# The first job of a hybrid attention layer in units of 2 chunks and 256 tokens

## What is computed

```python
h = concatenate([meta, x], axis=1)                    # 16 learned tokens + 512, width 1024
h = layer_norm(h, ln_emb_g, ln_emb_b)                 # over the 1024 features
proj = h @ w_in                                       # split into 11 parts:
(qa, ka, va, ga, qi, ki, wi, cq, ckv, kpe, gb) = split(proj)
# branch A: indexer scores from qi, ki, wi; top 128 keys per query; softmax with T5 bias
# branch B: latent attention, q from rms_norm(cq) @ w_uq, k and v from rms_norm(ckv) @ w_ukv
mixed = concatenate([oa * silu(ga), ob * silu(gb)])
out = layer_norm(ALPHA * h + mixed @ w_out, ln_post_g, ln_post_b)[:, 16:]
```

## Time and profile before

| | us |
|---|---|
| median of 3 runs (range) | 334.42 (333.64 to 335.16) |
| the profiled execution | 335.0 |
| its span, first to last instruction | 333.2 |
| TensorE busy | 319.4 (96%) |
| VectorE, ScalarE, GpSimd busy | 235.9, 174.6, 199.2 |

### The profile page before, as it was taken

One profiled execution on the slowest core, in us unless ns is written; L12 is line 12 of the kernel. 1 busy time (PEld: TensorE's weight loads), 2 busy tenths in 40 slices (PEclk: granted clock), 3 DMA queues, 4 the chain that ended last, 5 costly groups with the idle time before them and its releaser, 6 DMA issues.

```text
span 333.2 us, 6144 instructions
## 1 busy us (share of the span) xinstructions
PE 319.4 (96%) x2098; PEld 275.9 (83%) x2098; DVE 235.9 (71%) x626; ACT 174.6 (52%) x382; POOL 199.2 (60%) x240
## 2 busy tenths in 40 slices
PE   8799999999999999989999999999999999999990
PEld 7588987778787888878797988897978898998990
DVE  5784720259965699999995995478787866564686
ACT  4685754343543355467545664677587753722220
POOL 6260899988432251556633589699859582660552
PEclk9799999999999999999999999999999999999998
DMA  7455432428513033202400232222323110130033
GB/s 270 190 147 223 131 94 95 128 74 296 176 63 127 1 107 100 79 0 73 136 2 16 65 129 97 91 77 92 98 92 95 66 35 30 66 126 2 2 122 130
DMA packets 11710, 32.86 MB, mean 99 GB/s; under 512 B 2409, under 2 KB 2793, under 8 KB 11681
## 3 DMA queue, kind: packets, MB, share of 16 engines
q1 hardware_dynamic: 8944, 26.89, 23.7%
q10 hardware_dynamic: 2736, 5.59, 5.5%
HBM read 29.83 MB, written 4.81 MB: 104 GB/s over the span
## 4 chain that ended last, share of the span: by engine, by line
PE 82%; DVE 10%; issue 2%; DMA 2%; ACT 2%; SPq 1%; DVEq 0%
PE ps_j L1319 50%; PE ps_o L1579 6%; PE ps_s L1530 4%; PE ps_s L1534 3%; DVE iw L1146 3%; PE ps_t L1319 3%; PE ps_s L1503 2%; DVE top L1142 2%; PE ps_t L1549 2%; DMA iw<-in_onehot 2%; PE ps_j L1371 2%; PE ps_t L1554 2%; ACT pr L910 1%; PE ps_j L1419 1%; PE ps_j L1382 1%
## 5 line engine op out<-in xcount | busy, mean ns | idle before, releaser
L569 POOL TENSOR_TENSOR wl<-raw,wh 128x1024 fp32r<-128x1024 f32 (+2 forms) x33 | 78.1, 2374 | 56.9 <-ACT wh L576 56.8
L1319 PE MATMUL ps_j<-hh,wh 128*128 128x512 f32 (+2 forms) x216 | 75.2, 348 | 0.1
L1319 PE MATMUL ps_j<-hl,wh 128*128 128x512 f32 (+2 forms) x216 | 74.7, 346 | 0.0
L1319 PE MATMUL ps_j<-hh,wl 128*128 128x512 f32 (+2 forms) x216 | 74.4, 345 | 0.0
L705 POOL TENSOR_SCALAR pr<-pr,rden 128x528 f32<-128x528 f32 (+1 forms) x64 | 35.3, 572 | 42.5 <-DVE rden L1186 42.5
L1319 PEld LDWEIGHTS ps_j<-hh,wh 128*128 128x128 f32 (+1 forms) x216 | 40.3, 186 | 6.3 <-issue 0.5
L1319 PEld LDWEIGHTS ps_j<-hh,wl 128*128 128x128 f32 (+1 forms) x216 | 40.3, 187 | 5.1
L1319 PEld LDWEIGHTS ps_j<-hl,wh 128*128 128x128 f32 (+1 forms) x216 | 40.3, 186 | 5.1
L910 ACT ACTIVATE pr<-pr,mn 128x528 f32<-128x528 f32 (+1 forms) x64 | 36.0, 564 | 14.4 <-DVE mn L1175 14.3
L576 ACT ACTIVATE wh<-raw 128x1024 fp32r<-128x1024 f32 (+2 forms) x35 | 35.9, 1040 | 0.4 <-DMA raw<-in_weights 0.4
L723 POOL TENSOR_TENSOR bm<-bias,mask 128x144 f32<-128x144 f32 (+3 forms) x32 | 27.5, 895 | 0.0
(11 more groups left out here) (292 smaller groups left out, 832.8 us busy)
## 6 DMA issues: line engine op xcount, KB each, us to landing
raw<-in_weights SPq DMA_DIRECT2D x37, 512.0 KB, 3.3
bias_by_distance<-bias_vector ACTq DMA_DIRECT2D x1, 2624.0 KB, 12.7
bias<-bias_by_distance ACTq DMA_DIRECT2D x8, 264.0 KB, 2.9
res<-in_x SPq DMA_DIRECT2D x4, 512.0 KB, 5.2
out<-res SPq DMA_DIRECT2D x3, 512.0 KB, 2.6
pt<-in_ln_emb_g SPq DMA_DIRECT2D x1, 512.0 KB, 5.5
pt<-in_ln_emb_b SPq DMA_DIRECT2D x1, 512.0 KB, 6.5
q_b<-qpe ACTq DMA_DIRECT2D x8, 64.0 KB, 2.0
```

Source lines behind the costliest of these rows:

```text
L569: eng.tensor_tensor(ring_of(False, b), raw_of(b), ring_of(True, b).bitcast(F32), ALU.subtract).then_inc(done, 1)
L1319: last = pe.matmul(dst, a, b, start=n == 0 and part[0], stop=n == count - 1 and part[1])
```

## The change

- SP issues the meta tokens, tiles 0 and 1, the parameters and the table, tile 2, then the first halves (chunks 0 to 3) of weight blocks 0 and 1, tile 3, and their second halves; blocks from 2 on follow as before.
- Meta tokens and tile 0 are normalised by ScalarE; tiles 1 to 3 by VectorE, in two halves of 512 features each (`tensor_scalar`, subtract the mean, multiply by the inverse deviation, in place in SBUF). Statistics, roots and normalising are interleaved by hand.
- Block 0's first half is cast by ScalarE, block 1's by VectorE, both second halves by GpSimd; block 2's cast moves from ScalarE to GpSimd. The low parts of blocks 0 and 1 are made by GpSimd in four pieces of 2 chunks.
- The job runs in 8 units of 2 chunks x 256 tokens. A unit has its own bank of 512 columns, 4 transposes, gains and offsets (two operations of 256 columns, VectorE for units 1, 5, 7, ScalarE for the others), one cast, one low part, and 12 matmuls of 256 columns. Units 0 to 3 need tiles 0 and 1 alone, units 4 to 7 tiles 2 and 3. TensorE's order of spreads, high and low passes is written out.
- 30 filler transposes stand ahead of the meta tokens instead of 36; the other 12 are gone.
- The meta columns are made on VectorE behind the last unit's low part.

The core of the diff:

```diff
+FIRST_BLOCKS = 2
+GAIN_BY_DVE = [u in (1, 5, 7) for u in range(DC)]
@@ helpers
+        def unit(u):
+            i, a = u % 4, u // 4
+            return (2 * i, 2 * i + 1), slice(META + 256 * a, META + 256 * a + 256)
@@ SyncE
+            tile_in(0)
+            tile_in(1)
             sp.dma_start(gain[:, :], gains).then_inc(par_in, 16)
             sp.dma_start(rb[:, :], rel_bias).then_inc(par_in, 16)
             sp.dma_start(oh_sb, onehot).then_inc(oh_in, 16)
+            tile_in(2)
+            for half in range(2):
+                c = slice(4 * half, 4 * half + 4)
+                for b in range(FIRST_BLOCKS):
+                    sp.dma_start(raw[:, b, c, :], weights[b, :, c, :]).then_inc(raw_in[b] if half else first_in[b], 16)
+                if half == 0:
+                    tile_in(3)
@@ GpSimd
+            pool.wait_ge(w_first_act, 1)
+            pool.wait_ge(w_high_dve, 1)
+            first_low(0)
+            first_low(1)
+            for b in range(FIRST_BLOCKS):
+                pool.wait_ge(raw_in[b], 16)
+                pool.tensor_copy(wh[:, 4:8, b * P:b * P + P], raw[:, b, 4:8, :]).then_inc(w_high_pool, 1)
+            pool.wait_ge(w_high_pool, 2)
+            first_low(2)
+            first_low(3)
+            pool.wait_ge(raw_in[2], 16)
+            pool.tensor_copy(ring_of(True, 2), raw_of(2)).then_inc(w_high_pool, 1)
@@ ScalarE
+            deviation(0); normal(0, 2); deviation(1); normal(1, 4); deviation(2)
+            act.wait_ge(first_in[0], 16)
+            act.activation(wh[:, 0:4, 0:P], raw[:, 0, 0:4, :], ACT.Copy).then_inc(w_first_act, 1)
+            gains_of(0); high(0); high(1); deviation(3); gains_of(2); high(2); gains_of(3); deviation(4)
+            high(3); gains_of(4); high(4); high(5); gains_of(6); high(6); high(7)
@@ VectorE
+            def inverse(n, done):
...
+                else:
+                    for x in (0, 512):
+                        part = res[:, t, x:x + 512]
+                        dve.tensor_scalar(part, part, mv[:, t, 0:1], rstd[:, t:t + 1], ALU.subtract,
+                                          ALU.mult).then_inc(xn_dve, 1)
+            stat(0, 0); stat(0, 1); stat(1, 0); inverse(0, 1); stat(1, 1); stat(2, 0); inverse(1, 3)
+            stat(2, 1); stat(3, 0); inverse(2, 5)
+            dve.wait_ge(first_in[1], 16)
+            dve.tensor_copy(wh[:, 0:4, P:2 * P], raw[:, 1, 0:4, :]).then_inc(w_high_dve, 1)
+            gains_of(1); stat(3, 1); low(0); low(1); stat(4, 0); stat(4, 1); inverse(3, 6); low(2)
+            inverse(4, 7); low(3); gains_of(5); low(4); gains_of(7); low(5); low(6); low(7)
@@ TensorE
-            busy(36)
+            busy(30)
...
+            def high(u):
+                pe.wait_ge(h_high, u + 1)
+                for c in chunks:
+                    for k in range(2):
+                        pe.matmul(ps_j[:, k, a:a + 256], wh[:, c, k * P:k * P + P], hh[:, c, s], start=c == 0, stop=False,
+                                  skip_group_check=True)
+                pe.wait_ge(w_low, u % 4 + 1)
...
+            spread(0); spread(1); pe.wait_ge(xn_dve, 2); spread(2); spread(3)
+            high(0); high(1); low(0); low(1); high(2); high(3); low(2)
+            pe.wait_ge(xn_dve, 6)
+            spread(4); spread(5); low(3); spread(6); high(4); spread(7); low(4); high(5); low(5)
+            high(6); low(6); high(7); low(7)
             pe.wait_ge(meta_s, 4)
```

More of the change, by code:

```diff
@@ L763, in _, with deviation @@
-            act.wait_ge(par_in, 32)
[L764 to L774, removed]
+            def deviation(n):
+                t, r = TILES[n]
+                act.wait_ge(stats, n + 1)
+                act.activation(rstd[0:r, t:t + 1], mv[0:r, t, 1:2], ACT.Sqrt, bias=eps_ln[0:r, 0:1]).then_inc(root, 1)
@@ L953, in _, with stat @@
             dve.wait_ge(eps, 2)
[L956 to L959, removed]
+            def stat(n, half):
+                t, r = TILES[n]
+                src = x_meta if t == 4 else res[:, t, :]
+                if half == 0:
                     dve.wait_ge(x_in[t], 16)
[L961 to L967, removed]
+                dve.bn_stats(st[0:r, t, half, :], src[0:r, 512 * half:512 * half + 512]).then_inc(bn_s, 1)
+                if half == 1:
@@ new lines, in gains_of, with low @@
+            def gains_of(u):
+                dve.wait_ge(x_t, u + 2)
+                for n, c in enumerate(unit(u)[0]):
+                    half = hbank(u)[:, 256 * n:256 * n + 256]
+                    dve.tensor_scalar(half, half, gcol[:, c:c + 1], bcol[:, c:c + 1], ALU.mult,
+                                      ALU.add).then_inc(h_aff, 1)
+            def low(u):
+                chunks, s = unit(u)
+                dve.wait_ge(h_high, u + 1)
+                c = slice(chunks[0], chunks[1] + 1)
+                dve.tensor_tensor(hl[:, c, s], hbank(u).rearrange("p (c n) -> p c n", c=2), hh[:, c, s].bitcast(F32),
+                                  ALU.subtract).then_inc(h_low, 1)
@@ new lines, in low @@
+            def low(u):
+                chunks, s = unit(u)
+                a = 256 * (u // 4)
+                pe.wait_ge(h_low, u + 1)
+                for k in range(2):
+                    for c in chunks:
+                        last = pe.matmul(ps_j[:, k, a:a + 256], wh[:, c, k * P:k * P + P], hl[:, c, s], start=False,
+                                         stop=c == DC - 1, skip_group_check=True)
+                    if u == DC - 1:
+                        last.then_inc(job_mm, 1)
@@ new lines, in _ @@
+            pe.wait_ge(xn_act, 2)
+            pe.wait_ge(xn_dve, 1)
+            spread(0)
+            spread(1)
+            pe.wait_ge(xn_dve, 2)
+            spread(2)
+            spread(3)
+            high(0)
+            high(1)
+            low(0)
+            low(1)
+            high(2)
+            high(3)
+            low(2)
+            pe.wait_ge(xn_dve, 6)
+            spread(4)
+            spread(5)
+            low(3)
+            spread(6)
+            high(4)
+            spread(7)
@@ L1307, in _ @@
+            low(4)
+            high(5)
+            low(5)
+            high(6)
+            low(6)
+            high(7)
+            low(7)
             pe.wait_ge(meta_s, 4)
@@ L1376, in _ @@
                     if kind == "cq":
[L1377 to L1395, removed]
-                            pe.wait_ge(h_low, DC)
-                            for k in range(2):
-                                for w, x in ((wh, hh), (wl, hh), (wh, hl)):
-                                    last = pe.matmul(ps_j[:, k, :], w[:, DC - 1, k * P:k * P + P], x[:, DC - 1, META:T],
-                                                     start=False, stop=x is hl)
-                                last.then_inc(job_mm, 1)
                         continue
```

179 lines of the change are left out of this document (118 added, 61 removed).

## The result

| | before | after |
|---|---|---|
| median device time | 334.61 us (6 runs, 333.64 to 335.16) | 337.52 us (6 runs, 336.81 to 337.92) |
| profiled execution: time, span | 335.0, 333.2 us | 337.89, 336.0 us |
| start of the job after cq ("next job") | 30.18 us | 32.08 us |
| from there to the end of the span | 303.0 us | 303.9 us |

The change makes the kernel slower: ratio 1.0089, 95% interval 1.0070 to 1.0108.

A forecast was written before the change was run, and what follows sets the result against it. TensorE was taken as the bound, waiting for normalising before the first job. Next job at 31.5 instead of 30.2 us gave +1.35: span 334.5, median 335.8 us, range 332.2 to 337.8 (forecast's own 335.0 to 337.0).

The forecast's parts named there:

- rival 2: TensorE's clock falls to half around its holes: next job +2.6 to +3.0 us, 337.0 to 337.4 us; chance 0.18.
- The step that decides: VectorE's halves of tiles 2 and 3 wait for GpSimd's running SBUF operations, 4.2 us in all.
- The assumption on who goes next: A blocked VectorE operation goes ahead of GpSimd's next one, which then runs before VectorE's next.
- VectorE's halves: Normalising half a tile on VectorE, SBUF to SBUF, takes 0.42 us unhindered, bounds 0.41 and 0.82.
- The front: TensorE's first spread starts at 9.6 us instead of 14.14; the first high part is ready at 12.0.
- rival 4: TensorE's clock before 12.9 us stays whole: no change in the sum; no separate chance given.
- GpSimd's row: GpSimd's casts and low parts of the first weight blocks keep it busy from 10.6 to 21.4 us without a gap.
- From tile 3 to the next job: TensorE's spreads, low part 3 and units 4 to 7: 7.6 us plus 0.9 waiting; next job at 31.5.
- What sets 14.14 before: ScalarE's tile-by-tile normalising, ending at 14.09 us, holds TensorE's first spread in the old kernel.
- Nothing behind 31.5 is late: Later weight blocks are requested earlier, from 17.0 instead of 20.1 us, so nothing after the next job's start is late.
- Rival 1: VectorE's four halves are not held up: next job at 27.3 or 28.7, 331.6 or 332.9 us; chance 0.21.
- Rival 3: The weight blocks' half transfers arrive 1.3 us late: next job near 32.4, +2.2 us, 336.6 us; chance 0.08.

The follow-up runs named there:

- e2: Changed kernel with tiles 2 and 3 normalised on VectorE by a form reading the inverse deviation from PSUM: 334.37 us, ratio 0.9981.
- e1: Changed kernel with one more wait: GpSimd casts block 2 and makes its low part only after tile 3 is normalised: 335.04 us, ratio 0.9994.
- e4: Changed kernel with 28 filler transposes on TensorE ahead of the spreads for tokens 256 to 511: 337.03 us, ratio 1.0065.
- e5: Changed kernel run once more, unedited: 337.59 us, ratio 1.0071.
- e8: e2 with weight blocks 0 and 1 transferred whole ahead of tile 3 instead of in halves around it: 335.24 us, ratio 1.0004.
- e3: Changed kernel with tiles 2 and 3 normalised whole by ScalarE instead of VectorE: 334.04 us, ratio 0.9963.
- e6: Changed kernel, tile 2 on ScalarE, tile 3 on VectorE with deviation from PSUM, two second-half spreads ahead of low pass 2: 333.49 us, ratio 0.9954.
- e7: Kernel before the change with each 512-column matmul of cq split into two of 256: 334.50 us, ratio 0.9993.

## Why the prediction was right, and where its sizes were off

The mechanism is the forecast's, and it is shown. The number is near the end of the range: 337.52 lies above the forecast's own 335.0 to 337.0 and just above rival 2's 337.0 to 337.4, and "slower by over 0.5%" had 0.37 against 0.43 for "within". Two terms that the sum had too small, and a late landing that I don't book to the change, make nearly all of the 1.7 us between.

**The step that decides** held. Forecast: tile 2's halves end at 17.5 and 19.0, tile 3's at 21.8 and 22.2. Measured: 16.41 and 17.83, 19.09 and 21.56. VectorE came to tile 2 0.4 us earlier than forecast (15.36, not 15.8), within the first of the two low parts instead of the second, and so got through one GpSimd operation sooner. That bought little, because tile 3's second half then met block 2's low part all the same. Three halves waited, 3.5 us in all (forecast 4.2); the one that didn't is tile 3's first and not its second. The assumption on who goes next, the blocked operation ahead of GpSimd's next one, fits: GpSimd's cast and low part of block 2 are longer where VectorE gets in (1.23 and 2.47 against 1.04 and 2.37 in e2). e2 prices the step: 3.06 us of next job, of which 2.45 are tile 3's and 0.6 the clock's. The 2.45 are the 3.5 of waiting less 0.8 for e2's slower form and 0.2 by which e2 came to tile 2 later.

**VectorE's halves** were put at 0.42 us; they take 0.50. Hidden behind the wait here.

**The front** held: first spread at 9.67 (9.6), first high pass at 12.16 (12.0 to 12.4). The spreads ran at full clock, where half was thought possible: rival 4, without effect, as it said.

**GpSimd's row** held: forecast busy 10.6 to 21.4, measured 11.11 to 21.27; its casts of 128x512 were put at 0.60 and took 0.59 (1.17 for two), block 2's was put at 1.1 and took 1.04 where undisturbed.

**From tile 3 to the next job** the sum was too short: 9.3 us forecast (22.2 to 31.5), 10.5 measured (21.56 to 32.08). Half of the difference is the clock: forecast whole, granted 0.50 from 21.0 to 24.4, 0.6 us by e1 to e4 (0.9 in e5). That is the mechanism of rival 2, which was to cost 1.2 to 1.6. The stretch lasted the 3.4 us supposed there, but TensorE stood still in the first 0.6, and at full clock it waits 0.46 us for ScalarE's cast of unit 4 (e2, at 21.63), at half clock it doesn't (24.67 in the changed kernel). The rest, 0.6, stands in e2 at full clock too (9.91 from its tile 3): a pass of four matmuls behind a spread or a wait takes 0.54 to 0.58 (21.63 to 22.17 there), not 0.47, four times, 0.35 in all; what is left lies in the first spread (0.50, not 0.35) and the wait for unit 4. The trace of before had this already: five passes behind a spread take 0.54 to 0.56 there (18.78 to 19.32), which the prediction's 13.9 us of work leaves out; of the 2.1 us that it puts down to the clock, the four spreads up to 16.95 account for 1.4 (2.81 where 1.40 were counted).

**What sets 14.14 before.** The prediction names normalising, which ended at 14.09. The chain of before comes another way, from the wait for the one-hot table (until 10.64) through the T5 bias and the twelve fillers, which run right up to the spread: the two paths tie. Both are shorter in the changed kernel, so nothing hangs on it.

**"Nothing behind 31.5 is late"** failed by 0.4 and 0.9 us in two executions, both times by the landing of q_b, which varies without the change as well. So the 1.7 us between 335.8 and 337.52 are: next job 0.6 later than forecast, tail 0.9 longer, and 0.2 because the forecast put the median 0.6 below the profiled execution, where it lay 0.4 below.

**The rivals.** Rival 1 is refuted by the 2.47 and 3.02 us pairs; its world exists, though, as e2, where the next job came at 29.02 for the 28.7 worked out there. Rival 3 is refuted: the first casts and the first low parts began within 0.5 us of the forecast, and by e8 whole blocks would have been no better. VectorE as an engine with too much work is refuted by e1 and e2.

So the change has a gain in it, and gives more than that back. Without the hold-up the next job comes 1.2 us (e2) to 1.7 us (e3) earlier than before in the profiled executions; with it, 1.9 us later. Part of that gain is the clock's: e2 and e3 had no stretch at 0.50 there, before had one. By the ratios over all runs the gain is 0.4% in e3, some 1.2 us, and in e2, at 0.2%, not shown.

## What to carry to other kernels

Before moving an elementwise operation that reads and writes SBUF from ScalarE to VectorE, look at GpSimd's row in the same microseconds, and at the duration of the same form elsewhere, because the wait shows as busy time. Here the move cost nothing for tile 1 and 3.5 us of waiting for tiles 2 and 3. Where both must run, put one operand of VectorE's operation into PSUM (0.70 us instead of 0.50, but not held up in any of the five pairs of e2, e6 and e8), let ScalarE do it, or hold back the GpSimd work that nobody waits for, as block 2's here. A first start that is 4.5 us earlier is worth nothing if the last input of the same stage comes later.

## What was not expected of the hardware

- The half clock isn't tied to the change. Near the start seven of the ten profiled executions have one stretch of 3.4 us at 0.50, but its place differs: 12.9 to 16.3 before, 21.0 to 24.4 and 22.5 to 25.9 in two executions of the changed kernel, 11.6 to 15.0 in e1, 9.6 to 13.0 in e4, 9.7 to 13.1 in e6, 12.0 to 15.4 in e7; e2, e3 and e8 had none from 6 to 34 us, with much the same work on TensorE. A forecast of the order of 0.6 us that rests on the clock's place is not to be had from one profile.
- VectorE's held-up form and GpSimd delay each other: GpSimd's cast of 1024 elements took 1.23 us instead of 1.04, its low part 2.47 instead of 2.37, where a half of VectorE's that had waited went in ahead of it.
- Transfers of 64 KB, alike in all kernels, landed after 2.0 us in some executions and 2.4 to 3.1 in others, and the scores that wait for them move by 0.4 to 0.9 us.
